# A fused two-block network on one core: the first layer norm taken one token tile at a time, and GpSimd's work on the normed rows spread out

## The reference, cut to what matters

```python
y = (y * silu(z)) @ w_out                      # a_w_out: 1024 x 2048
x = layer_norm(4 ** 0.25 * x + y, ln_g[0], ln_b[0])
kv = (x @ kv_w)                                # 2048 x 3072: k and v, compressed, selected, window
# k_c and v_c are compressed by cmp_w1 and cmp_w2; x is needed again for x @ b_w_in,
# and as natural rows for the residual of the next layer norm, some 700 us later
```

## Time and profile before

| | before |
|---|---|
| median of 3 runs | 2164.67 us (2164.65 to 2164.68) |
| the profiled execution: time | 2167.36 us |
| the profiled execution: span | 2165.6 us |
| PE busy | 2062.2 us, 95% |
| PEld busy | 1809.4 us, 84% |
| DVE busy | 1305.3 us, 60% |
| ACT busy | 970.5 us, 45% |
| POOL busy | 65.9 us, 3% |
| granted TensorE clock, mean | 0.983 |

### The profile page before, as it was taken

The page is one execution under the profiler, slowest core; times in us unless marked ns, Lnnn a source line. Parts: engine busy times, 40 slices in busy tenths (PEclk is TensorE's granted clock), DMA queues, the critical chain, the costliest instruction groups (busy, mean ns, idle before and its releaser), DMA issues.

```text
span 2165.6 us, 32848 instructions
## 1 busy us (share of the span) xinstructions
PE 2062.2 (95%) x12838; PEld 1809.4 (84%) x12838; DVE 1305.3 (60%) x1761; ACT 970.5 (45%) x1381; POOL 65.9 (3%) x69
## 2 busy tenths in 40 slices
PE   6999889999999999896999999899999999999997
PEld 6898689898988888786889887788888888888886
DVE  7788775456666656557555655555555555655654
ACT  5554344344444444334345545554434434443443
POOL 2000130000000000000000000100000000000000
PEclk9999999999999999998999999999999999999999
DMA  8334556645455554663545444456566566556652
GB/s 258 98 108 153 171 182 216 183 127 157 145 155 152 148 156 140 203 194 98 156 126 174 152 132 146 165 172 189 193 192 184 194 194 191 185 195 186 192 191 92
DMA packets 198849, 359.85 MB, mean 166 GB/s; under 512 B 21440, under 2 KB 29824, under 8 KB 198080
## 3 DMA queue, kind: packets, MB, share of 16 engines
q1 hardware_dynamic: 196928, 352.01, 52.4%
q0 software_dynamic: 1600, 5.96, 0.9%
q10 hardware_dynamic: 192, 0.05, 0.0%
HBM read 355.88 MB, written 2.10 MB: 165 GB/s over the span
## 4 chain that ended last, share of the span: by engine, by line
PE 49%; issue 39%; DVE 8%; ACT 2%; DMA 1%; POOL 0%; SPq 0%; DVEq 0%; POOLq 0%; ACTq 0%
PE acc L469 22%; PE acc L473 18%; DVE w_low L1537 2%; PE banks L737 1%; ACT w_high L992 1%; PE banks L823 1%; PE banks L766 1%; PE banks L692 1%; PE banks L569 1%; DMA raw<-in_a_w_in 1%; PE banks L752 0%; PE banks L842 0%; PE banks L548 0%; PE banks L826 0%; DVE x_high_low L1564 0%
## 5 line engine op out<-in xcount | busy, mean ns | idle before, releaser
L1537 DVE TENSOR_TENSOR w_low<-raw,w_high 128x1024 fp32r<-128x1024 f32 x656 | 805.8, 1234 | 685.9 <-ACT w_high L992 684.5
L992 ACT ACTIVATE w_high<-raw 128x1024 fp32r<-128x1024 f32 x656 | 691.4, 1058 | 781.4 <-PE acc L469 347.5
L473 PE MATMUL acc<-x_high_low,w_high 128*128 128x256 f32 x2560 | 378.4, 287 | 9.0 <-DVE w_low L1537 8.9
L473 PEld LDWEIGHTS acc<-x_high_low,w_high 128*128 128x128 f32 x2560 | 338.2, 194 | 11.7 <-issue 10.3
L469 PE MATMUL acc<-w_high,x_high_low 128*128 128x512 f32 x1152 | 323.9, 394 | 4.0 <-ACT transposed_tmp L1345 4.0
L469 PEld LDWEIGHTS acc<-w_high,x_high_low 128*128 128x128 f32 x1152 | 211.6, 188 | 47.3 <-issue 3.7
L473 PE MATMUL acc<-x_high_low,w_low 128*128 128x256 f32 x1280 | 207.5, 285 | 0.0
L469 PE MATMUL acc<-w_high,h_high 128*128 128x512 f32 x576 | 180.7, 395 | 6.3 <-DVE w_low L1537 3.8
L469 PE MATMUL acc<-w_low,h_high 128*128 128x512 f32 x576 | 178.9, 392 | 0.0
L469 PE MATMUL acc<-w_high,h_low 128*128 128x512 f32 x576 | 178.9, 392 | 0.0
L473 PEld LDWEIGHTS acc<-x_high_low,w_low 128*128 128x128 f32 x1280 | 178.5, 194 | 0.0
(11 more groups left out here) (342 smaller groups left out, 2078.0 us busy)
## 6 DMA issues: line engine op xcount, KB each, us to landing
raw<-in_b_w_in SPq DMA_DIRECT2D x128, 512.0 KB, 3.8
raw<-in_w_mlp_in SPq DMA_DIRECT2D x128, 512.0 KB, 3.7
raw<-in_w_mlp_out SPq DMA_DIRECT2D x128, 512.0 KB, 3.6
raw<-in_w_in SPq DMA_DIRECT2D x96, 512.0 KB, 4.1
raw<-in_kv_w SPq DMA_DIRECT2D x48, 512.0 KB, 4.1
raw<-in_a_w_in SPq DMA_DIRECT2D x32, 512.0 KB, 4.9
raw<-in_b_w_out SPq DMA_DIRECT2D x32, 512.0 KB, 3.9
raw<-in_w_out SPq DMA_DIRECT2D x32, 512.0 KB, 3.7
```

The source lines that it names most:

```text
L473: ins_ = nc.tensor.matmul(ACC[pair][:, m // 2, (m % 2) * TOK:(m % 2 + 1) * TOK], wa[:, k, j, m * P:(m + 1) * P], xa[:, kt + j, :], start=f ...
L992: nc.scalar.activation(WH[:, s % SPLIT, :, :], RAW[:, s, :, :], ACT.Copy).then_inc(hi_ready, 1)
L1537: V.tensor_tensor(WL[:, k, :, :], RAW[:, p % SLOTS, :, :], WH[:, k, :, :].bitcast(F32), ALU.subtract).then_inc(lo_ready, 1)
```

## The change

**PE.** Group c=3 of a_w_out is run tile by tile (`tiles_apart`): tick 52 to 55 for tile t=0 (24 matmuls), then the same four ticks for t=1; `slot_used` counts only in the second pass, and a new semaphore `tile_full` marks the end of the first. A portion of the turn is now one token tile and four k-tiles (`tile_turn`): 8 portions (t, b). PE turns (0,0) to (0,3), then (1,0) and (1,1), and starts tick 56; (1,2) stands behind tick 57 and (1,3) behind tick 59, inside the unit. Ticks wait for the splits of both tiles (`tiles_ready`).

**DVE.** The residual and statistics of c=2 come behind the low of tick 55 and no longer behind that of tick 58. Then tile 0's last residual, statistics, epsilon and norm, the low of tick 56, tile 1's, and then splits, norms and lows by turns in a written order.

**ACT.** `tile_turned` takes a portion in four instructions of 128 columns (before: two of 256). The highs of ticks 59, 60 and 61 stand behind portions 3, 5 and 6. The order of portions for ACT and DVE is `TURN_ORDER`.

**POOL.** `rsqrt` is run once for each tile. The natural rows are taken in 16 operations of 128x512, each behind a wait for `slot_used`: from tick 59 on, one operation for two ticks, the last at tick 89.

Semaphore counts of later stages are renumbered to fit (`rows_ready`, `rstd_rows`).

```diff
+TURN_ORDER = [(0, 0), (0, 1), (1, 0), (1, 1), (0, 2), (1, 2), (0, 3), (1, 3)]
...
+        def tiles_apart(unit, pair, kt0, start, xh, xl):
+
+            for t in range(NT):
+                for s in range(SPLIT, SLOTS):
+                    if t == 0:
+                        pe.wait_ge(lo_ready, unit * SLOTS + s + 1)
+                    for j in range(2):
+                        kt = kt0 + 2 * (s - SPLIT) + j
+                        for n, (xa, wa) in enumerate(((xh, WH), (xh, WL), (xl, WH))):
+                            ins_ = nc.tensor.matmul(PAIRS[pair][:, t, :], xa[:, kt, t * P:(t + 1) * P], wa[:, s % SPLIT, j, :],
+                                                    start=start and s == SPLIT and j == 0 and n == 0,
+                                                    stop=s == SLOTS - 1 and j == 1 and n == 2)
+                    if t:
+                        ins_.then_inc(slot_used, 1)
+                if t == 0:
+                    ins_.then_inc(tile_full, 1)
+
+        def tile_turn(first, t, b):
+
+            if t:
+                pe.wait_ge(tr_tmp, first + TURN_ORDER.index((0, b)) + 1)
+            pe.wait_ge(tile_rows, 4 * t + b + 1)
+            for j in range(4):
+                kt = 4 * b + j
+                ins_ = nc.tensor.transpose(BK[b][:, j * P:(j + 1) * P], X[:, t, kt * P:(kt + 1) * P], ID)
+            ins_.then_inc(tr_full, 1)
+
+        def tiles_ready(first):
+            return lambda s: pe.wait_ge(split_done, first + TURN_ORDER.index((1, s // 2)) + 1) if s % 2 == 0 else None
...
-        for c in range(4):
+        for c in range(3):
             gemm(U_AOUT + c // 2, G_AOUT + c, "rows", HH, HL, s0=4 * (c % 2), s1=4 * (c % 2) + 4, kt0=CB,
-        transposes(TR_X1, X, lambda i: pe.wait_ge(rows_ready, 1 + i // 2))
-        gemm(U_KV, G_KV, "cols", ready=split_ready(TR_X1))
+        pe.wait_ge(acc_free, G_AOUT + 2)
+        tiles_apart(U_AOUT + 1, (G_AOUT + 3) % 2, CB, True, HH, HL)
+        for b in range(4):
+            tile_turn(TR_X1, 0, b)
+        for b in range(2):
+            tile_turn(TR_X1, 1, b)
+        def later_turns(s):
+            if s in (1, 3):
+                tile_turn(TR_X1, 1, 2 + s // 2)
+        gemm(U_KV, G_KV, "cols", ready=tiles_ready(TR_X1), extras=later_turns)
...
-        turned(TR_X1, gain=0, bias=16)
+        def tile_turned(first, m, gain, bias):
+
+            t, b = TURN_ORDER[m]
+            act.wait_ge(tr_full, first + 4 * t + b + 1)
+            if m >= 2:
+                act.wait_ge(split_done, first + m - 1)
+            for j in range(4):
+                kt = 4 * b + j
+                ins_ = nc.scalar.activation(TMP[:, m % 2, :, :].rearrange("p j t -> p (j t)")[:, j * P:(j + 1) * P],
+                                            BK[b][:, j * P:(j + 1) * P], ACT.Identity,
+                                            scale=PT[:, 0, gain + kt:gain + kt + 1], bias=PT[:, 0, bias + kt:bias + kt + 1])
+            ins_.then_inc(tr_tmp, 1)
+        for m in range(8):
+            tile_turned(TR_X1, m, 0, 16)
+            if m in (3, 5, 6):
+                high(0)
...
+        def tile_residual(t, chunk, group, alpha):
+
+            xr = X[:, t, chunk * COLS:(chunk + 1) * COLS]
+            ins_ = V.scalar_tensor_tensor(xr, xr, alpha, ACC[group % 2][:, t, :], ALU.mult, ALU.add)
+            if t:
+                ins_.then_inc(acc_free, 1)
+                v.wait_ge(acc_free, group + 1)
+            else:
+                steps.link(ins_)
+            steps.link(V.bn_stats(STATS[:, t, chunk, :], xr))
+            steps.link(V.bn_aggr(MV[:, t, :], STATS[:, t, :, :]))
+            V.tensor_scalar(MS[:, t:t + 1], MV[:, t, 1:2], LN_EPS, None, ALU.add, ALU.bypass).then_inc(ms_rows, 1)
+
+        def tile_normed(t, c):
+
+            xr = X[:, t, c * COLS:(c + 1) * COLS]
+            V.tensor_scalar(xr, xr, MV[:, t, 0:1], RSTD[:, t:t + 1], ALU.subtract, ALU.mult).then_inc(tile_rows, 1)
+
+        def tile_split(first, m):
+
+            t, b = TURN_ORDER[m]
+            v.wait_ge(tr_tmp, first + m + 1)
+            high_, low_ = (x[:, 4 * b:4 * b + 4, t * P:(t + 1) * P] for x in (XH, XL))
+            split(high_, low_, TMP[:, m % 2, :, :].rearrange("p j (h q) -> p (j h) q", h=2))
...
         v.wait_ge(x_loaded, 16)
-        for c in range(4):
+        for c in range(3):
             if c % 2 == 0:
-                low(0, SLOTS)
+                low(0, SLOTS if c == 0 else SLOTS - LEAD)
             residual(SLOTS * (U_AOUT + c // 2) + 4 * (c % 2) + 4, (G_AOUT + c) % 2, c, ALPHA)
             chunk_stats(c, G_AOUT + c)
-        whiten(1, rows_ready)
-        split_turned(TR_X1)
+        v.wait_ge(tile_full, 1)
+        tile_residual(0, 3, G_AOUT + 3, ALPHA)
+        v.wait_ge(rstd_rows, 1)
+        for c in range(4):
+            tile_normed(0, c)
+        low(0)
+        v.wait_ge(slot_used, SLOTS * U_KV)
+        tile_residual(1, 3, G_AOUT + 3, ALPHA)
+        tile_split(TR_X1, 0)
+        v.wait_ge(rstd_rows, 2)
+        tile_normed(1, 0)
+        tile_normed(1, 1)
+        tile_split(TR_X1, 1)
+        tile_split(TR_X1, 2)
+        low(0)
+        tile_normed(1, 2)
+        tile_normed(1, 3)
+        tile_split(TR_X1, 3)
+        low(0)
+        for m in range(4, 7):
+            tile_split(TR_X1, m)
+            low(0)
+        tile_split(TR_X1, 7)
...
             if half == 0:
-                rsqrt(1)
+                rsqrt(1, 0, 1)
+                rsqrt(2, 1, 2)
                 pool.wait_ge(tr_full, TR_X1 + 8)
...
-            for t in range(NT):
-                steps.link(GP.tensor_tensor(X[:, t, cols], X[:, t, cols], GB[:, 0, :], ALU.mult))
-                ins_ = GP.tensor_tensor(X[:, t, cols], X[:, t, cols], GB[:, 1, :], ALU.add)
-                if half and t:
+            for n in range(4):
+                t, part_ = n % 2, slice(n // 2 * COLS, (n // 2 + 1) * COLS)
+                xr = X[:, t, half * DM // 2 + n // 2 * COLS:half * DM // 2 + (n // 2 + 1) * COLS]
+                pool.wait_ge(slot_used, U_KV * SLOTS + 3 + 16 * half + 4 * n)
+                steps.link(GP.tensor_tensor(xr, xr, GB[:, 0, part_], ALU.mult))
+                pool.wait_ge(slot_used, U_KV * SLOTS + 5 + 16 * half + 4 * n)
+                ins_ = GP.tensor_tensor(xr, xr, GB[:, 1, part_], ALU.add)
+                if half and n == 3:
```

More of the change, by code:

```diff
@@ L316, in build @@
     rows_ready = sem("rows_ready")
+    tile_full, tile_rows = sem("tile_full"), sem("tile_rows")
     out_ready = sem("out_ready")
@@ L781, in group @@
                 gemm(g * 4 + (U_NSA + 4), g * 4 + (G_NSA + 4), "cols", parity=0)
-            pe.wait_ge(rows_ready, g + 5)
+            pe.wait_ge(rows_ready, g + 1)
             for i in range(2):
@@ L798, in _ @@
                  ready=(lambda s: pe.wait_ge(split_done, TR_Y + s + 1)) if u == 0 else None)
-        transposes(TR_H, HN, lambda i: pe.wait_ge(rows_ready, 9 + i // 2))
+        transposes(TR_H, HN, lambda i: pe.wait_ge(rows_ready, 5 + i // 2))
         def rotate(n):
@@ L1280, in kvc_high @@
                                      ACC[(G_KV + n) % 2][:, b, :].rearrange("p (h t) -> p h t", h=2), ACT.Copy).then_inc(act_part, 1)
-        unit()
+        unit(ticks=SLOTS - 3)
         unit(first=lambda: kvc_high(0))
@@ L1901, in chunk_stats, with whiten @@
                 steps.inc(V.bn_stats(STATS[:, t, chunk, :], X[:, t, chunk * COLS:(chunk + 1) * COLS]))
-        def whiten(n, rows_sem):
+        def tile_residual(t, chunk, group, alpha):
[17 more added lines that the diff above has]
+            split(high_, low_, TMP[:, m % 2, :, :].rearrange("p j (h q) -> p (j h) q", h=2))
+        def whiten(n):
             steps.wait()
@@ L1914, in whiten @@
                 for t in range(NT):
[L1915 to L1924, removed]
+                    steps.inc(V.scalar_tensor_tensor(xc[:, t, :], xc[:, t, :], MV[:, t, 0:1], gain, ALU.subtract, ALU.mult))
                 steps.wait()
@@ L2115, in _ @@
         v.wait_ge(gain_in, 96)
-        whiten(2, x_rows)
+        whiten(3)
         def root_mean_squares(n, squares, dst):
@@ L2138, in root_mean_squares @@
                         steps.inc(ins_)
-        root_mean_squares(3, 4, HN)
+        root_mean_squares(4, 4, HN)
         split_turned(TR_H)
@@ L2353, in _ @@
         v.wait_ge(gain_in, 112)
-        root_mean_squares(4, 12, None)
+        root_mean_squares(5, 12, None)
     @block.gpsimd
@@ L2378, in _, with rsqrt @@
         GP.memset(DECAY[:, :, :, 0:1], 0.0).then_inc(zeroed, 1)
-        def rsqrt(n):
+        def rsqrt(n, t0=0, t1=NT):
             pool.wait_ge(ms_rows, n)
-            GP.tensor_tensor(RSTD[:, 0:NT], MS[:, 0:NT], MHALF[:, 0:NT], ALU.pow).then_inc(rstd_rows, 1)
+            GP.tensor_tensor(RSTD[:, t0:t1], MS[:, t0:t1], MHALF[:, t0:t1], ALU.pow).then_inc(rstd_rows, 1)
         def gains(dst, name, layer, cols):
@@ L2413, in _ @@
         pool.dma_start(GW[:, :, :], B_IN[:, ZW * 4:ZW * 4 + GATES].rearrange("(k p) n -> p k n", p=P)).then_inc(gw_in, 16)
```

(6 more changed lines are left out.)

## The result

The changed kernel takes 2152.32 us (median of 5 runs, 2151.3 to 2154.1) against 2164.68 us of the kernel before (5 runs, 2164.65 to 2166.24): 12.4 us less, ratio 0.994, 95% interval [0.9928, 0.9953]. The profiled execution took 2151.43 us with a span of 2149.6.

The account below looks back on a forecast made before the run. PE, 95% busy, was taken to bound the kernel, so only its idle or slow places could give time. 6.4 + 6.0 - 0.7 + 0.7 = 12.4 us off the median 2164.67 gave 2152.3 us, range 2147.3 to 2158.5.

Parts of the forecast that it names:

- Two passes over ticks 52 to 55 cost nothing: Last a_w_out group: same 48 matmuls, first pass ends near 245.4, second near 250.85, no wait, no cost.
- DVE's order: Before the turns: c=2 residual and statistics move under the passes; tile 0's norm ends at 250.3, ahead of PE's 250.85.
- The turn up to tick 56: Hole before the first kv_w matmul: tick 56 starts at 258.3 instead of 264.72, 6.4 us gained.
- Inside the unit: First kv_w unit: stall before tick 59 disappears, 6.0 us gained; two turns of 0.36 between ticks lose 0.7.
- POOL: Natural rows: about 1.3 us per 512-column operation; nothing on PE in kv_w, nothing or at worst 3 us in w1.
- (c): Rival, w1 unit: POOL's pieces reach PE, up to 3 us, 2155.3; 6%.
- (d): Rival: the lock or late lows make each of POOL's 16 operations hold PE by over 1.03 us, kernel slower; 3%.
- The reason that I gave for the splits: Around the last turn: POOL's first operation comes after all turns (271), so no split meets one.
- The clock: After 258.3: 4 us at half clock lose 2.0, against 2.7 lost behind the old second hole; 0.7 gained.
- Rival (a): Hole before tick 56: turns break idle time, clock doesn't fall, 2.0 more, 2150.3; support: clock kept over 262 to 278; 17%.
- Rival (b): Turns: ACT's narrow copies and run-wise splits cost upper bounds, tick 56 starts 1.6 later, two more stalls, 2155.5; 14%.
- (e): Rival: a wait between queues leaves a stall of the old size, gain only 3 us, 2161.7; 4%.

Follow-up runs that it names:

- second group: The changed kernel run again unchanged, beside the kernel before on one chip: 2152.0 us, 13.9 us below the kernel before.
- the two small parts: Kernel before with only DVE's earlier c=2 residual and statistics and POOL's 16 spread operations, both tiles' norm and turn together: 2154.9 us.
- one pass: Changed kernel with the last a_w_out group in one pass as before, both tiles in every tick: 2157.5 us.
- PE kept busy: Changed kernel plus 18 and 18 idle matmuls, results unused, behind tile 0's turns and tile 1's first two turns: 2151.9 us, again 2151.2 us.

## Why the prediction was right

The time came out as forecast, and so did the mechanism, part by part. That the median met 2152.3 to within 0.1 us is luck: the interval of the ratio allows 10.2 to 15.6 us, the second group measured 13.9, and in the first profile two terms were off by 0.4 and 0.5 us in opposite ways. By its steps:

- *Two passes over ticks 52 to 55 cost nothing*: shown. The passes run at one matmul in 0.227 us, and without them 5.6 to 5.9 us are lost.
- *DVE's order*: tile 0's norm ended 0.9 us ahead of PE (0.55 forecast); residual and statistics of c=2 alone give 2.1 us.
- *The turn up to tick 56* (6.4 us): 7.69 us from the end of a_w_out in the first profile, 7.23 in four more runs of the same code, 7.3 forecast; 6.0 to 6.5 us gained. ACT's portion took 1.45 (1.5 forecast), the split 1.1. In the first profile the clock fell at 253.7, under the second turns, whose eight transposes took 1.94 us; in the second it fell only at 257.1 and they took 1.09. I had let it fall behind 258.3, that is behind the start of tick 56.
- *Inside the unit* (6.0 us): no idle time at all, as forecast. The two turns cost 0.36 each.
- *POOL*: 1.30 us for an operation, as forecast, where no low was in its way, and up to 1.99 where one was; in the w1 unit two lows took 3.01 us of a pair of ticks of 3.58, and PE did not wait. Rivals (c) and (d) fall. The reason that I gave for the splits holds only just: the last split stands behind the last turn, so POOL's first operation does not come after all splits. It ended at 272.87, and the last split began at 273.06.
- *The clock* (0.7 us): 2.0 us lost forecast; inside the unit it was 1.3 to 1.5 in the two profiles of the changed kernel, and 2.6 lay behind the second hole of before (2.7 forecast). The gain is 1.0 to 1.2, not 0.7, and smaller by up to 1.2 in other runs of the same code.
- Rival (a) did not happen by itself, and what I had put for it was weak: 4.4 of the 5.6 idle us over 262 to 278 are the start of the second hole, and the clock fell in that hole, at 278.2. Rival (b) fell on ACT's pace, (e) on PE's timeline.

In the first profile this adds up to 6.0 + 6.0 - 0.7 + 1.2 = 12.5 us.

What the sum of parts hid is that they replace each other. POOL's spread alone gives 8.6, the tile order alone 7.4, both 12.5: in the tile order the last turn comes late, so POOL begins late too and meets only the last split and the lows. Behind the two small parts (10.7) the tiles bring 1.8 us of stretch; by their times these two kernels can't be told apart (their intervals overlap).

## What to carry to other kernels

Where an engine's work beside the path shares a resource with one on the path, first cut that work into pieces and place them by the progress of the path; here that gave 8.6 of 12.5 us by itself, and 5.0 behind the tile order. A norm by tile pays only if the product in front of it is finished by tile as well. Half clock behind a hole cost time here only where PE set the pace right after it (nothing over the first turns, 1.3 us and more over kv_w ticks), so look at what lies under it before filling the hole.

## What was not expected of the hardware

- ACT's copies of 128 columns last 471 ns each (32 of them in the trace) but come one in 0.363 us (8 in 2.90), so the duration of one overstates the pace. The Trainium skill's "ScalarE: Activation LUTs" (its section "What ACT_TABLE_LOAD costs") gives 186 ns, 93 ns for each pointer operand and 0.833 ns for a column, with an overlap of 93 ns between instructions. An estimate by that page is 479 ns for one copy and a pace of 386 ns, close to both.
- Transposes alone brought the clock back: in the trace of before PE ran only transposes from 258.26 and the clock was at 0.95 over 261 to 262, 1.00 behind it; with both small parts they ran from 255.18 and the clock was at 0.88 over 258 to 259. The Trainium skill's "TensorE: Matmul & The Clock Gate" (its part 4, "PE-mode transpose") says that the full clock doesn't engage for transposes; here it did.
- The granted clock of parts that are the same in both kernels differs from execution to execution. The start of the stretch lay between 249.03 us ("one pass", clock 1.00 over 80 to 100 us) and 253.10 ("PE kept busy", 0.84 over 80 to 90 and 0.82 over 90 to 100).
